# First block: early condition chunks in column tiles, q, kv, u and v as three products of parts

## The reference

```python
cond = jax.nn.silu(c)
for l in range(DEPTH):
    mod = cond @ w_ada[l] + b_ada[l]
    shift1, scale1, gate1, shift2, scale2, gate2 = jnp.split(mod[:, None, :], 6, axis=-1)
    h = x * (1 + scale1) + shift1
    p = h @ w_in[l]            # q 512, k 128, v 128, z 1024 (u and v halves), gates a and b 2048 columns
    ...                        # attention on q, k, v; gelu, layer norm and w_spatial on z
    y = (sigmoid(gate_a) * (o_a @ w_branch_a) + sigmoid(gate_b) * (o_b @ w_branch_b)) @ w_out
    x = layer_norm(ALPHA * x + gate1 * y, ln1_g[l], ln1_b[l])
    h = x * (1 + scale2) + shift2
    x = layer_norm(ALPHA * x + gate2 * moe_ffn(h, ...), ln2_g[l], ln2_b[l])
```

## Time and profile before

| | us |
|---|---|
| median of 3 runs | 3822.88 (3820.14 to 3823.03) |
| the profiled execution | 3822.81 |
| its span | 3820.9 |
| PE, DVE, ACT, POOL busy | 3397.0, 1660.0, 829.7, 602.2 |
| mean granted clock of TensorE | 0.924 |

### The profile page before, as it was taken

The page is one execution under the profiler, slowest core; times in us unless marked ns, Lnnn a source line. Parts: engine busy times, 40 slices in busy tenths (PEclk is TensorE's granted clock), DMA queues, the critical chain, the costliest instruction groups (busy, mean ns, idle before and its releaser), DMA issues.

```text
span 3820.9 us, 45626 instructions
## 1 busy us (share of the span) xinstructions
PE 3397.0 (89%) x18903; PEld 2369.8 (62%) x18903; DVE 1660.0 (43%) x2757; ACT 829.7 (22%) x1162; POOL 602.2 (16%) x556
## 2 busy tenths in 40 slices
PE   7988999996978899999498878878989986988799
PEld 3755343332656343333398768776989885878498
DVE  1424333334434333332645564543545456554454
ACT  1211111110130111111233421212333343211132
POOL 4501333331630233333100000000000000000000
PEclk9988999998978999999699979988999997899899
DMA  8546999998744999999653300013555430010452
GB/s 283 202 170 272 394 385 389 385 383 337 265 168 175 376 388 381 381 385 384 245 195 112 127 23 18 27 67 109 196 175 181 150 127 23 1 45 23 143 183 94
DMA packets 305399, 799.21 MB, mean 209 GB/s; under 512 B 57030, under 2 KB 155868, under 8 KB 251308
## 3 DMA queue, kind: packets, MB, share of 16 engines
q1 hardware_dynamic: 245804, 727.16, 50.5%
q0 software_dynamic: 58848, 67.05, 5.3%
q10 hardware_dynamic: 544, 2.10, 0.1%
HBM read 989.01 MB, written 53.48 MB: 273 GB/s over the span
## 4 chain that ended last, share of the span: by engine, by line
PE 83%; DVE 10%; DMA 2%; ACT 2%; issue 2%; SPq 0%; POOL 0%; DVEq 0%; POOLq 0%; ACTq 0%
PE f_bank L811 17%; PE s_bank L2091 14%; PE f_bank L832 8%; PE s_bank L2128 6%; PE f_bank L772 4%; PE f_bank L893 3%; PE s_bank L2287 2%; PE s_bank L2171 2%; PE f_bank L792 2%; PE s_bank L2078 2%; PE s_bank L2302 2%; PE s_bank L2159 2%; PE s_bank L2398 2%; PE s_bank L2297 2%; PE f_bank L981 2%
## 5 line engine op out<-in xcount | busy, mean ns | idle before, releaser
L811 PE MATMUL f_bank<-f_ringA,f_arena 128*64 128x512 f32 x3072 | 685.5, 599 | 15.0 <-DMA f_ringA<-in_w_up,f_chosen 14.9
L811 PEld LDWEIGHTS f_bank<-f_ringA,f_arena 128*64 128x64 f32 x3072 | 216.1, 138 | 404.1 <-issue 402.8
L2091 PE MATMUL s_bank<-s_hT_high_parts,s_highA_parts 128*128 128x256 f32 x1408 | 403.2, 286 | 25.6 <-DVE s_hT_parts L2647 25.6
L2091 PE MATMUL s_bank<-s_hT_parts,s_highA_parts 128*128 128x256 f32 x1408 | 402.6, 286 | 0.0
L2091 PE MATMUL s_bank<-s_hT_high_parts,s_ringA_parts 128*128 128x256 f32 x1408 | 402.4, 286 | 0.0
L832 PE MATMUL f_bank<-f_ringB,f_arena 128*64 128x512 f32 x1536 | 346.1, 592 | 2.1 <-DVE f_arena L1598 2.1
L1583 DVE TENSOR_TENSOR f_arena<-f_arena,f_bank 128x256 f32<-128x256 f32 x96 | 58.8, 613 | 589.6 <-ACT f_arena L1193 589.6
L2091 PEld LDWEIGHTS s_bank<-s_hT_high_parts,s_highA_parts 128*128 128x128 f32 x1408 | 274.7, 195 | 28.3 <-issue 26.9
L1114 ACT ACTIVATE f_arena<-f_bank 128x512 f32<-128x512 f32 (+1 forms) x266 | 144.8, 583 | 608.8 <-PE f_bank L792 277.2
L2091 PEld LDWEIGHTS s_bank<-s_hT_parts,s_highA_parts 128*128 128x128 f32 x1408 | 274.8, 195 | 1.4
L2091 PEld LDWEIGHTS s_bank<-s_hT_high_parts,s_ringA_parts 128*128 128x128 f32 x1408 | 274.5, 195 | 0.0
(11 more groups left out here) (420 smaller groups left out, 5807.7 us busy)
## 6 DMA issues: line engine op xcount, KB each, us to landing
f_ringA<-in_w_gate SPq DMA_DIRECT2D x128, 1024.0 KB
f_ringA<-in_w_up SPq DMA_DIRECT2D x128, 1024.0 KB
f_ringB<-in_w_down SPq DMA_DIRECT2D x128, 1024.0 KB
s_ringA<-in_ffn_in SPq DMA_DIRECT2D x88, 1024.0 KB, 7.7
f_ringA<-in_w_ada SPq DMA_DIRECT2D x46, 1024.0 KB, 13.2
s_arena<-in_ffn_out SPq DMA_DIRECT2D x44, 1024.0 KB, 6.5
s_ringA<-in_w_in SPq DMA_DIRECT2D x40, 1024.0 KB, 6.2
f_ringA<-in_w_in SPq DMA_DIRECT2D x28, 1024.0 KB, 13.1
```

The lines of the kernel that those rows point to most:

```text
L811: last = mm(ps[j * CAP:(j + 1) * CAP, :].rearrange("p (h c) -> p h c", h=2), picked[:, b % 2, k, j * CAP:(j + 1) * CAP], gu[j][:, :, k, :] ...
L2091: last = mm(ps[:, t * S:(t + 1) * S], parts_of(wx[:, k, cs_]), parts_of(hx[:, k, :]), start=(k == 0 and x == 0), stop=(k == DT - 1 and x = ...
```

## The change

Six edits, all in the first block:

- SyncE's start: the identity and the small rows first, then x, then the four early condition chunks, then the other constants. GpSimd issues its parameter loads only when the last early chunk has landed (layer 0). TensorE waits for the identity alone at first.
- `early_ada`: each chunk's 512 columns are four tiles of 128, product (k, t) in column tile t, so a chunk fills all four tiles, chunk by chunk in both layers; three turnings instead of four.
- `stream`: ada8 moves from behind in0 to behind in2.
- q, kv, u, v: three products of parts. New are the buffers `high_q` (also for v), `high_kv`, `high_u`, `hT_high`, `hT_low`; ScalarE's `first_up`, `in_up` and `mod_in`; VectorE's subtractions. The low part of w is written over the chunk. For q the three products run one after the other over both token halves, for the rest they alternate.
- Layer end: ScalarE takes the early rows before the last root and makes layer 1's first high part; VectorE's `take_early` moves ahead of the norm.
- `sel` moves to another buffer.

```diff
-        sel = parts_of.part("sel", arena, arena_at, 7680, 768).rearrange("p (b m s) -> p b m s", b=3, m=MT)
+        sel = hid_high[:, :, :].rearrange("p a b -> p (a b)")[:, 0:768].rearrange("p (b m s) -> p b m s", b=3, m=MT)
+        high_q = parts_of.part("high_q", arena, arena_at, 6144, 4096).rearrange("p (k c) -> p k c", k=DT)
+        high_kv = parts_of.part("high_kv", arena, arena_at, 12544, 2048).rearrange("p (k c) -> p k c", k=DT)
+        high_u = ringB[:, 2:4, :].rearrange("p a (k c) -> p (a k) c", k=4)
+        in_highs = [high_q, high_kv, high_u, high_q]
+        hT_high, hT_low = [ringB[:, n, :].rearrange("p (k s) -> p k s", k=DT) for n in range(2)]
...
-        stream += [("in", 0), ("ada", 8), ("in", 1), ("in", 2), ("in", 3), ("ada", 9), ("in", 4), ("ada", 4),
+        stream += [("in", 0), ("in", 1), ("in", 2), ("ada", 8), ("in", 3), ("ada", 9), ("in", 4), ("ada", 4),
...
+                    sp.dma_start(consts["ident"][:, :], a["const_ident"]).then_inc(consts["ident_landed"], 16)
...
+                    for m in range(MT):
+                        sp.dma_start(x_tok[:, m, :], a["x"][0].rearrange("(m p) d -> p m d", p=P)[:, m, :]
+                                     ).then_inc(consts["x_landed"], 16)
                     for c in range(third):
                         early_ada(0, c)
+                    constants("cos", "sin", "jlt", "moe")
...
+                if l == 0:
+                    pool.wait_ge(ada_landed[third - 1], 32)
...
-                if l:
-                    for c in range(third):
-                        pe.wait_ge(ada_landed[c], 32 * l + 32)
-                steps = [(c, k) for k in range(DT) for c in range(third)] if l else \
-                    [(c, k) for c in range(third) for k in range(DT)]
-                for c, k in steps:
-                    if l == k == 0:
-                        pe.wait_ge(ada_landed[c], 32)
-                    last = mm(ps[32 * c:32 * c + 32, :], cond[:, k:k + 1].broadcast_to([P, 32]), ada_place(l, c)[:, k, :],
-                              start=(k == 0), stop=(k == DT - 1))
-                    if c < third - 1 and k == DT - 1:
+                for c in range(third):
+                    pe.wait_ge(ada_landed[c], 32 * l + 32)
+                    w = ada_place(l, c)
+                    for k in range(DT):
+                        for t in range(4):
+                            last = mm(ps[32 * t:32 * t + 32, c * P:(c + 1) * P], cond[:, k:k + 1].broadcast_to([P, 32]),
+                                      w[:, k, t * P:(t + 1) * P], start=(k == 0), stop=(k == DT - 1))
+                    if c < third - 1:
                         last.then_inc(ada_used, 1)
                 banks.fill(last, ("ada rows", l))
                 banks.evacuated(pe, ("ada rows", l))
                 pe.nop().then_inc(ada_used, 1)
                 ps = banks.claim(pe, ("ada cols", l))
-                for t in range(4):
-                    last = turn(ps[:, t * P:(t + 1) * P], ada_rows[:, t * P:(t + 1) * P], ident[:, :])
+                for c in range(third):
+                    last = turn(ps[:, c * P:(c + 1) * P], ada_rows[:, c * P:(c + 1) * P], ident[:, :])
...
+                pe.wait_ge(first_high, l + 1)
                 for b in range(4):
                     banks.evacuated(pe, ("xT", b))
-                for c, name in enumerate(("q", "kv", "u", "v")):
-                    width = 2 * KVW if name == "kv" else 512
-                    w = rows8(slotA(a_in[c]))
-                    landed(a_in[c])
-                    for m in range(MT):
+                wide = [(m, m * P, (m + 1) * P) for m in range(MT)]
+                ps_of = [banks.claim(pe, ("q", m)) for m in range(MT)]
+                for m, lo, hi in wide:
+                    for k in range(DT):
+                        mm(ps_of[m][:, :], parts_of(hT_high[:, k, lo:hi]), parts_of(high_q[:, k, :]),
+                           start=(k == 0), stop=False)
+                pe.wait_ge(h_low, 4)
+                for m, lo, hi in wide:
+                    for k in range(DT):
+                        mm(ps_of[m][:, :], parts_of(hT_low[:, k, lo:hi]), parts_of(high_q[:, k, :]),
+                           start=False, stop=False)
+                pe.wait_ge(in_low, 1)
+                for m, lo, hi in wide:
+                    for k in range(DT):
+                        last = mm(ps_of[m][:, :], parts_of(hT_high[:, k, lo:hi]), parts_of(in_chunk(0)[:, k, :]),
+                                  start=False, stop=(k == DT - 1))
+                    banks.fill(last, ("q", m))
+                for c, name in ((1, "kv"), (2, "u"), (3, "v")):
+                    w, high = in_chunk(c), in_highs[c]
+                    width = w.shape[2]
+                    pe.wait_ge(in_low, c + 1)
+                    for m, lo, hi in wide:
                         ps = banks.claim(pe, (name, m))
                         for k in range(DT):
-                            last = mm(ps[:, 0:width], hT[:, k, m * P:(m + 1) * P], w[:, k, 0:width],
-                                      start=(k == 0), stop=(k == DT - 1))
+                            for x, (hx, wx) in enumerate(((hT_high, high), (hT_low, high), (hT_high, w))):
+                                last = mm(ps[:, 0:width], parts_of(hx[:, k, lo:hi]), parts_of(wx[:, k, :]),
+                                          start=(k == 0 and x == 0), stop=(k == DT - 1 and x == 2))
...
+            def mod_in(bank):
+                ps = banks.read(act, ("xT", bank))
+                for t in range(2):
+                    j = 2 * bank + t
+                    for dst in (hT[:, j, :], parts_of(hT_high[:, j, :])):
+                        last = f(dst, ps[:, t * S:(t + 1) * S], ACT.Identity,
+                                 bias=mod[:, j:j + 1], scale=modp1[:, DT + j:DT + j + 1])
+                banks.free(last, ("xT", bank))
+
+            def first_up(l):
+
+                a_filled(act, a_first, l)
+                f(parts_of(high_q), in_chunk(0), ACT.Copy).then_inc(first_high, 1)
+
+            def in_up(c):
+
+                a_filled(act, a_in[c], l)
+                if c == 3:
+                    banks.read(act, ("q", 1))
+                f(parts_of(in_highs[c]), in_chunk(c), ACT.Copy).then_inc(in_high, 1)
...
+                    first_up(0)
                 act.wait_ge(early_mod, l + 1)
                 for b in range(2):
-                    modulate("xT", b, 0, DT)
+                    mod_in(b)
+                for c in (1, 2):
+                    in_up(c)
                 for m in range(MT):
                     take(("q", m), p_tok[:, m, 0:QW], lambda ps: ps[:, :])
+                in_up(3)
...
+                if l + 1 < DEPTH:
+                    take(("ada rows", l + 1), ada_rows, lambda ps: ps[:, :])
                 roots(4, MT)
                 if l + 1 < DEPTH:
-                    take(("ada rows", l + 1), ada_rows, lambda ps: ps[:, :])
+                    act.wait_ge(y_room, 1)
+                    first_up(l + 1)
...
-                    modulate("xT", b, 0, DT)
+                    ps = banks.read(dve, ("xT", b))
+                    for t in range(2):
+                        j = 2 * b + t
+                        for dst in (hT[:, j, :], parts_of(hT_high[:, j, :])):
+                            last = ts(dst, ps[:, t * S:(t + 1) * S], modp1[:, DT + j:DT + j + 1],
+                                      mod[:, j:j + 1], ALU.mult, ALU.add)
+                    banks.free(last, ("xT", b))
+                for b in range(4):
+                    banks.evacuated(dve, ("xT", b))
+                    two = slice(2 * b, 2 * b + 2)
+                    tt(parts_of(hT_low[:, two, :]), hT[:, two, :], parts_of.value(hT_high[:, two, :]), ALU.subtract
+                       ).then_inc(h_low, 1)
+                dve.wait_ge(first_high, l + 1)
+                for c in range(4):
+                    if c:
+                        dve.wait_ge(in_high, c)
+                    tt(parts_of(in_chunk(c)), in_chunk(c), parts_of.value(in_highs[c]), ALU.subtract).then_inc(in_low, 1)
...
-                norm_x(4, ln2_landed, 2, y_sum)
                 if l + 1 < DEPTH:
                     take_early(l + 1)
+                norm_x(4, ln2_landed, 2, y_sum)
```

33 lines of the change are left out of this document (19 added, 14 removed).

## The result

| | before | after |
|---|---|---|
| median of 4 runs, us | 3822.95 | 3844.25 (3841.05 to 3848.35) |
| ratio, with 95% interval | | 1.0053 (1.0040 to 1.0065) |
| the profiled execution, its span | 3822.8, 3820.9 | 3843.2, 3841.4 |
| mean granted clock | 0.924 | 0.915 |

The change costs 21 us. The forecast was 3831, its range ended at 3840: the direction was right, the size was not, and the range missed.

The account below looks back on a forecast made before the run. TensorE was taken as the bound before, GpSimd's chain ahead of the spatial product after; -2.0 us (layer 0) + 7.5 (layer 1) + 3 (clock) = +8.5 us on 3822.9, forecast 3831 us, range 3815 to 3840.

Parts of the forecast that it names:

- Bound and chain: Ahead of the spatial product: GpSimd's sums of ada8 and ada9, then ada5's load, sum and VectorE's copies (15.25 us), set its start.
- Rival 3: Ahead of the spatial product: GpSimd's chain is no bound, TensorE keeps 10.3 and 6.7 us; 3806 us, chance 0.05.
- rival 1: GpSimd's sums ahead of the spatial product: not held up, 24.3 us each; about 3815 us, chance 0.12.
- Rival 2: GpSimd's sums beside VectorE's long subtractions: the lock takes half, 1.8 us each; 3823 us, chance 0.15.
- Rival 4: Early condition rows: column tiles of 128 columns don't overlap, 6.9 us or more a chunk; 3836 us, chance 0.06.
- Rival 5: Loads or splits come later, TensorE waits inside u or v, ada8 lands at 60; 3838 us, chance 0.12.
- Layer 0 up to sv: Layer 0 up to the spatial product: it starts at 129.0, 2.0 us earlier than 131.03.
- The long subtractions: VectorE's subtractions of in2 and in3 beside GpSimd's sum of ada8: 3.6 us lost each, or 7 us per layer.
- The clock behind the idle time: TensorE after idling ahead of the spatial product: half clock, about 1.5 us per layer (0 to 3).
- Layer 1 up to sv: Layer 1 up to the spatial product: it starts at 1051.7, 7.5 us later than 1044.18.
- The seam: Between the layers: `take_early` costs the same 0.4 us ahead of the norm; first high part (3.6 us) lies beside it.
- The sum: Whole kernel: -2.0 for layer 0, +7.5 for layer 1, +3 for the clock, total +8.5 us.

Follow-up runs that it names:

- e5: Changed kernel with VectorE's subtraction of the weight chunks cut to 64 columns, low parts of w_in left out; ratio to the kernel before 0.9998.
- e4: Changed kernel with VectorE's sum of chunk ada5 moved behind the copies of wsT and the spatial gate; ratio to the kernel before 1.0031.
- e10: Changed kernel with 24 overwritten 128x256 products on TensorE in its idle time, between the turnings of q and k; ratio to the kernel before 1.0046.
- e1: Kernel before with only the new start and the column tiles, plain products and old order of loads; ratio to the kernel before 0.9985.
- e3: Changed kernel with ada8 moved back to second place in the loads, behind in0; ratio to the kernel before 1.0047.
- e6: Changed kernel with 24 overwritten 128x256 products on TensorE behind the turning of q and k, after the idle time; ratio to the kernel before 1.0101.
- e8: Kernel before with the new start and column tiles, plus ada8 moved behind in2 in the loads; ratio to the kernel before 1.0000.

## Why the prediction was wrong

**Bound and chain: right.** Sv is released by VectorE's copy, behind sum 5, behind the load of ada5, behind GpSimd, in both layers. e5 and e4 each take one link out, and sv moves to 121 and 119. Rival 3 (no bound) and rival 1 (no hold-up) fell. Rival 2 (half of the hold-up) fell as well: two losses of 3.6 us a layer were forecast against its 1.8, and 7.2 and 7.1 us were lost. Rival 4 fell too: the column tiles take 3.0 to 3.6 us a chunk, and 3.5 was forecast. Rival 5 was small: TensorE waited 0.7 us inside v in layer 0 and 1.9 us inside u and v in layer 1, and ada8 came at 56.2.

**Layer 0 up to sv: right, to the tenth by luck.** q at 46.0 (48.1), gates at 87.8 (89.2), ada8 at 56.2 (58), sum of ada8 31.0 us (31.5), sv at 129.03 (129.0). Two errors cancel: ada8 came 1.8 us earlier, and the sum of ada9 took 26.1 us instead of 24.3.

**The long subtractions: right in size.** 2.45 and 4.7 us, 7.2 together, where two times 3.6 were forecast. The Trainium skill's page "SBUF — State Buffer" (section "Who interferes with whom") says that the later of the two is blocked fully, and the trace now shows it at 4.4 us: the operation of 72.51 is longer by 4.70 us, more than a whole subtraction (4.43). Where less was lost, 2.45 us, GpSimd had come 1.8 us late into one that was running. So the full 4.4 us for every subtraction would have been too much here, as the forecast's even 3.6 was too little for one and too much for the other.

**The clock behind the idle time: the step that failed.** I put it at "about 1.5 us per layer (0 to 3)". From sv to branch it is 98.5 us instead of 92.4 in layer 0 and 98.4 instead of 93.3 in layer 1, so 6.1 and 5.1: +8.2 us on the forecast, all outside its own bound. TensorE's idle time in this stretch did not grow (18.8 us against 19.1 in layer 0, 20.6 against 21.9 in layer 1), so what grew is the time of its instructions. 4.0 us in each layer arise at once: sv takes 6.93 us instead of 3.68, the eight single-column products behind it 1.81 instead of 1.00, and the first scores start 8.5 us behind sv instead of 4.5. That alone is outside the bound of 3.

I had looked at the clock behind one idle stretch ahead of q, where products of 128x512 follow. In the changed kernel the clock is back 5 us after q's start (50.9). Behind the idle stretch ahead of sv come 128x64 products, single columns and 64x256 scores, and it is back only at 143.0 in layer 0 and 1078.1 in layer 1, 15 and 16 us after TensorE went on, some 4 us after the gates of 128x256 had begun.

e5 shows both together in layer 0: with 7 us less hold-up the idle stretch is 1.7 us instead of 9.1, and the 6.4 us behind sv are gone as well. In layer 1 of e5 the idle stretch and the slow sv remain, and so do all but 0.5 us of the stretch behind it. e10 gives back 4.0 and 2.1 us by keeping TensorE busy. The other 2.1 and 1.1 us are not shown to come from the idle stretch: kernels whose sv runs at the full clock and whose sum 5 stands in its old place need 91.2 to 96.5 us to branch (e1, e3, e6, e8, e10), as the clock rises and falls in the heads in every kernel. The changed kernel less its 4.0 us, 94.5 and 94.4, lies among them.

**Layer 1 up to sv: too small by 4.** Forecast 1051.7, 7.5 later; measured 11.7 later from the seam. The first sum starts 2.0 us later from the seam than forecast, probably since in1, in2 and ada8 share their time with the parameters, which no run tested; and the two sums take 57.6 us instead of 55.6. The end of v is 4.4 us earlier from the seam, not 6.7; it hides in the same wait.

**The seam: neutral, as assumed.** Between branch and seam it takes 3.0 us more than before, and the kernels scatter by 5.2 us there.

**The sum.** 8.5 forecast, +8.2 for the stretch behind sv, +4 for layer 1: 21, measured 20 to 21. Of the 8.2, 5.0 are shown to be the clock behind the idle time (two times 4.0, less the 3 forecast). That it closes so well owes something to the seam and the end, where +3.0 and -3.3 us cancel. Bounding the clock by 3 us a layer also made the range too narrow at the top.

**What I had not costed** is the change's own first step. I wrote that q starts at 48.1 "as today", but not that plain products could have begun at 39. e1 shows it: the start alone is worth 6 us, and in layer 0 the parts save 1.3 us of TensorE's time up to the gates and use up the 7 us that the start had won.

## What to carry to other kernels

When a faster engine runs into a chain on other engines, cost the wait twice: as a wait, and as the clock behind it, by what stands behind it. Here an idle stretch with 128x64 products, single columns and the first scores behind it left TensorE at 1.2 GHz for 15 us, until larger products had come; with 128x512 or 128x256 products behind it the clock was back after 5 to 6 us. Before an engine's step is made faster, put the sums and loads that aren't needed yet behind it (here one sum and the order of the loads turned +20 us into -8, though the new start alone gives -6); and a long VectorE instruction of two SBUF operands belongs nowhere beside a GpSimd chain that someone waits for.
